# A two-layer streaming encoder on one Trainium2 core: ScalarE loads one table set for logarithm and exponential ahead of the norms of each stage

## The reference, cut to what matters

```python
def rms_norm(x, g):
    y = xf * lax.rsqrt(jnp.mean(xf * xf, axis=-1, keepdims=True) + RMS_EPS)
    return (y * g.astype(jnp.float32)).astype(x.dtype)

def layer(x, ...):
    m, ... = token_mix(rms_norm(x, ng[NORM_MIX_PRE]), ...)   # attention heads and RWKV-7 heads
    x = x + rms_norm(m, ng[NORM_MIX_POST])
    c = cross_attend(rms_norm(x, ng[NORM_X_PRE]), mem_k, mem_v, w_q, w_o)
    x = x + rms_norm(c, ng[NORM_X_POST])
    f = swiglu(rms_norm(x, ng[NORM_FFN_PRE]), w_gu, w_dn)
    x = x + rms_norm(f, ng[NORM_FFN_POST])
```

## Time and profile before

| | |
|---|---|
| median of 3 runs | 4215.57 us (4213.71 to 4216.14) |
| span of the profiled execution | 4217.2 us |
| TensorE busy | 3606.6 us (86%) |
| VectorE busy | 1806.6 us (43%) |
| ScalarE busy | 1447.4 us (34%) |
| GpSimd busy | 128.0 us (3%) |
| table loads on ScalarE | 121, of 1283 ns each |

### The profile page before, as it was taken

The page is one execution under the profiler, slowest core; times in us unless marked ns, Lnnn a source line. Parts: engine busy times, 40 slices in busy tenths (PEclk is TensorE's granted clock), DMA queues, the critical chain, the costliest instruction groups (busy, mean ns, idle before and its releaser), DMA issues. The chain is left out here.

```text
span 4217.2 us, 86503 instructions
## 1 busy us (share of the span) xinstructions
PE 3606.6 (86%) x32960; PEld 3336.0 (79%) x32960; DVE 1806.6 (43%) x2729; ACT 1447.4 (34%) x2667; POOL 128.0 (3%) x188
## 2 busy tenths in 40 slices
PE   4889779987887999999749796899688889999995
PEld 3878647766787999999749784677588789999994
DVE  3345346533654333333451453555345543333334
ACT  3334344433554111111342343444245531111115
POOL 0000000001000000000000100000001000000000
PEclk6999869887998999999979896899799899999997
DMA  5111111105641111111131112101175311111111
GB/s 170 52 55 62 61 36 42 65 23 187 210 170 36 46 45 49 45 45 45 36 107 41 59 62 61 36 25 65 36 256 212 105 36 45 45 45 47 43 50 51
DMA packets 249818, 306.36 MB, mean 73 GB/s; under 512 B 27252, under 2 KB 203844, under 8 KB 248480
## 3 DMA queue, kind: packets, MB, share of 16 engines
q1 hardware_dynamic: 232320, 225.61, 16.9%
q0 software_dynamic: 17184, 76.45, 4.8%
HBM read 231.01 MB, written 71.00 MB: 72 GB/s over the span
## 5 line engine op out<-in xcount | busy, mean ns | idle before, releaser
L779 PE MATMUL PS<-HH,WH 128*128 128x352 f32 (+3 forms) x3712 | 1240.7, 334 | 125.3 <-PEq L763 125.3
L779 PE MATMUL PS<-HH,WL 128*128 128x352 f32 (+3 forms) x3712 | 1211.8, 326 | 0.0
L779 PE MATMUL PS<-HL,WH 128*128 128x352 f32 (+3 forms) x3712 | 1209.5, 326 | 0.0
L779 PEld LDWEIGHTS PS<-HH,WH 128*128 128x128 f32 x3712 | 719.3, 194 | 147.0 <-issue 141.8
L779 PEld LDWEIGHTS PS<-HH,WL 128*128 128x128 f32 x3712 | 719.3, 194 | 3.0 <-issue 0.3
L779 PEld LDWEIGHTS PS<-HL,WH 128*128 128x128 f32 x3712 | 716.8, 193 | 0.0
L2326 DVE TENSOR_TENSOR WL<-WRAW,WH 128x1024 fp32r<-128x1024 f32 x194 | 241.2, 1243 | 659.0 <-DVEq L2325 659.0
L1515 ACT CAST WH<-WRAW 128x1024 fp32r<-128x1024 f32 x218 | 228.6, 1049 | 608.1 <-ACTq L1520 564.5
L1479 PE MATMUL PS<-GH,WH 128*128 128x352 f32 x1056 | 342.0, 324 | 0.0
L1479 PE MATMUL PS<-GH,WL 128*128 128x352 f32 x1056 | 340.9, 323 | 0.0
L1479 PE MATMUL PS<-GL,WH 128*128 128x352 f32 x1056 | 340.8, 323 | 0.0
(11 more groups left out here) (336 smaller groups left out, 4929.7 us busy)
## 6 DMA issues: line engine op xcount, KB each, us to landing
WRAW<-in_w_gate_up SPq DMA_DIRECT2D x88, 512.0 KB, 3.7
W<-split_dram SPq DMA_DIRECT2D x48, 512.0 KB, 4.5
WRAW<-in_w_down SPq DMA_DIRECT2D x46, 512.0 KB, 3.2
WH<-split_dram SPq DMA_DIRECT2D x40, 512.0 KB, 3.7
WL<-split_dram SPq DMA_DIRECT2D x40, 512.0 KB, 4.6
WRAW<-in_w_in SPq DMA_DIRECT2D x38, 512.0 KB, 3.7
raw_dram<-MIX SPq DMA_DIRECT2D x24, 528.0 KB, 3.1
R<-raw_dram SPq DMA_DIRECT2D x24, 512.0 KB, 3.5
```

Source lines behind the costliest of these rows:

```text
L779: ins = e.matmul(out, lhs(k, wp), rhs(k, xp), start=first, stop=(k == n - 1 and xp == 1))
```

## The change

ScalarE's program gets a helper that loads the set `natural_log_exp_and_others`, and calls it at six places: ahead of the memory squares, in every pair at its fourth tile pair, in the RWKV prologue behind the sigmoids, at the start of the output projection, in the first FFN half behind its first SiLU, and behind the last FFN half. Nothing else of the program is touched; which loads are put in when it is built follows from the set that is in place.

```diff
+        def roots_ahead():
+
+            e.preload_act_table_set("natural_log_exp_and_others")
+
...
             e.wait_ge(S("memT_act"), 1)
             e.sem_inc(S("memT_act"), -1)
+            roots_ahead()
             squares(R2, MEM)
             highs(in_tmp, MEM)
...
                 for n, (u, x0) in enumerate(tile_pairs(j)):
                     by_token(u, x0)
                     by_token(u, x0 + 1)
+                    if n == 3:
+                        roots_ahead()
                     if n < 3:
                         lora(ahead, 2 * n)
...
             lora(0, 0, 1, 2, 3, 4, 5)
+            roots_ahead()
             key_row(0)
             key_squares(0)
             decays(0)
...
+            roots_ahead()
             for half in range(2):
                 copy(HH[:, 4 * half:4 * half + 4, part_span(0)], R2[:, 4 * half:4 * half + 4, part_span(0)]).then_inc(S("hh_ready"), 1)
...
             def first_half():
                 silu(0)
+                roots_ahead()
                 stat(2, 2)
...
             half(0)
             half(1)
+            roots_ahead()
             squares_out(0)
```

## The result

The changed kernel takes **4169.33 us** (median of 4 runs, 4165.29 to 4172.42), the kernel before beside it 4215.85 us (4213.71 to 4223.21): ratio 0.9888, 95% interval 0.9870 to 0.9907. The forecast was 4166 us, with a range of 4144 to 4192. The profiled execution of the changed kernel took 4172.42 us, its span is 4170.8.

A forecast was written before the change was run, and what follows sets the result against it. TensorE, busy 86% of 4217.2 us, was taken as the bound; ScalarE edits pay only where TensorE waits for it. Fifteen terms summed to 24.6 us per layer, 49.2 for both, forecasting 4166 us, range 4144 to 4192.

The forecast's parts named there:

- Term 1: Memory norm: two loads go (2.6 us), an explicit one comes ahead of the first square (1.3); gain 1.3 us per layer.
- Term 9: Projection's first norm: TensorE waits 0.71 us and about as long again for banks ScalarE returns late; gain 1.3 per layer.
- term 10: Two norms around 1071 to 1081: four loads go, the copy between waits for its product; gain 3.2 us per layer.
- Term 12: Norm in the back projection: TensorE waits 3.10 us for a bank, about 1 stays; gain 2.1 us per layer.
- Term 13: Norms at 1265 and 1270: the copies between wait for products; gain 3.2 us per layer.
- term 15: Last FFN half: six loads go, one comes in an idle stretch, VectorE sets the end; gain 0.
- rival B: Shortened TensorE waits leave its clock at 2.4 GHz, each saving 1 to 3 us: 4150 us; chance 0.09.
- A: Weight transfers are late next from output projection to back projection, losing 12.4 us per layer: 4191 us; chance 0.12.
- D: Loads are still put before Ln and Exp, so the 18 explicit ones only add: 4226 us; chance 0.03.
- F: Earlier copies and casts meet VectorE or a transfer everywhere, nothing passed on: within 0.2% of 4216 us; chance 0.02.
- E: A drain behind each load exists and hides in what follows, terms twice as large: 4117 us; chance 0.02.
- C: Slower by TensorE's clock in RWKV stretches, each us at 1.2 GHz costing up to 0.46: 4295 us; chance 0.03.

The follow-up runs named there:

- experiment 5: Unedited repeats: changed kernel 4158.23 and 4161.68 us, kernel before 4222.44 us; changed kernel with each explicit load written twice, one of two kept, 4156.75 us.
- experiment 3: Changed kernel without the explicit load behind the last FFN half: 4158.09 us, ratio 0.9861 to the kernel before.
- experiments 4: Changed kernel, memory load moved to the loop's head, prologue load into the wait for the decays, projection's and pair 3's loads left out: 4156.00 us.
- experiment 6: Changed kernel with a load of the exponential's set directly ahead of every explicit load, 57 loads: 4167.62 us, ratio 0.9906 to the kernel before.
- experiment 8: Changed kernel with explicit loads moved off the path or left out, run again beside the changed kernel's third lot: 4147.58 us, ratio 0.9854 to the kernel before.
- experiment 2: Changed kernel whose explicit load at the output projection names the exponential's set, so 36 loads return through the back projection: 4195.14 us, ratio 0.9948 to the kernel before.

## Why the prediction was right, and where its steps were not

The measured time lies 3.3 us above the forecast in its own lot; over the four lots (17 runs, 4149.44 to 4172.42) the changed kernel stands at 0.9861 to 0.9888 of the kernel before, that is 4157 to 4169 by 4215.85 us. The range holds all of that, and the forecast of 4166 lies in the upper half of what was measured. The mechanism is the one forecast: 104 loads went, and the time fell where ScalarE was the late one. That the total came so near is in part luck, as the terms show: some are too large, some too small, and the clock gave and took in places where the sum had nothing.

Outside the RWKV pairs the sum had 24.6 - 0.9 - 2.5 = 21.2 us per layer, 42.4 in all; the traces show 3433.2 - 3387.1 = **46.1**. In the pairs it had 6.8; the traces show 785.9 before (mean of two, both layers) and 784.3, 769.1, 768.3 and 778.0 after: between 1.6 and 17.6. Term by term, from the matched instructions of the first traces of both kernels (first layer, then second where it differs):

| term | forecast | measured | |
|---|---|---|---|
| 1 memory norm | 1.3 | -0.3 (2.56 gained, 2.82 lost ahead of it, 0.33 of that already ahead of the first load); 1.45 (2.56, 1.11) | a load at the loop's head, exposed in the first layer |
| 2 mix norm | 2.0 | 2.1; 1.6 | |
| 3 tanh | 0 | 0 | |
| 4 RWKV prologue | 2.6 | 2.67; 2.81 | |
| 5 pair 0 | 0.9 | 0.8; 0.95 | |
| 6 pair 4 | 2.5 | 2.46 (wait 3.10 to 0.64) | |
| 7 sample norm | 2.6 | 2.56 | |
| 8 load at the projection | -1.3 | -1.28 | |
| 9 first norm | 1.3 | 0.2 | step failed |
| 10 norms in a row | 3.2 | 3.57 | |
| 11 | 2.6 | 2.56 | |
| 12 back projection | 2.1 | 2.24 of wait, 3.4 with what follows; 4.8 | clock, see below |
| 13 norms in a row | 3.2 | 4.5; 4.1 | under-sized |
| 14 first FFN half | 1.6 | 1.36 (wait 6.30 to 4.94) | |
| 15 last FFN half | 0 | 0 | but see term 1 |

The terms don't account for all of the 46.1. In the first layer 25.4 us come outside the pairs; 3.4 of them are the attention part, by the clock (experiment 5). In the second layer 21.0 come: behind term 14 the changed kernel is 49.2 us ahead, at the end of the program 46.3, and what it loses in that FFN I didn't take apart. One slip stands in the sum itself: term 10 adds 0.7 and 2.6 and writes 3.2.

**Term 9** is a step that failed. These rows of the kernel before, three of the projection and the first load of term 13, I had not weighed:

```profile
1042.04 0.33 PE L779 MATMUL PS<-HL,WH 128*128 128x384 f32 x1
...
1042.37 0.53 ACT L2033 ACTIVATE TMP<-TMP 128x384 f32<-128x384 f32 x1
...
1042.80 0.46 ACT L1515 COPY R<-PS 128x384 f32<-128x384 f32 x1
...
1265.48 1.28 ACT L2029 ACT_TABLE_LOAD   x1 [6.68 <-ACTq L2028]
```

I took the 0.71 us of TensorE's wait, "and about as long again", for ScalarE's delay, since the copy stood with no idle time behind the Exp. But the product that this copy takes out (the 128x384 of L779) ended only at 1042.37, and the copy began at 1042.80. After, where ScalarE stands idle for 2.38 us ahead of that copy, the product ends at 1032.79 and the copy starts at 1032.99, 0.20 us behind it. So ScalarE had been late by about 0.2 us of the 0.43, and that is what came: the wait fell from 0.71 to 0.50, and the next one, the "as long again" (0.65 us at 1044.80), is still 0.65. I had asked for the product's end in terms 10, 12 and 13, not here.

**Term 13** is mis-sized. I let the first of the two norms pass on 0.7 us, because the copy between would wait for its product. From the first Ln's slot to the cast before lie 9.69 us (load at 1265.48, cast at 1275.17), after 5.16 (1246.12 to 1251.28): of four loads, 5.13 us, 4.5 are passed on, 2.55 and 1.96 by the two norms. The copy between the norms now waits 0.53 us for its product, so that much is lost; I had put the loss at 1.9.

**Term 12** has its wait right (2.24 us against 2.1) but not what follows it. Behind the wait of 3.10 us TensorE soon ran at 1.2 GHz; behind the wait of 0.86 that is left it did so for a shorter time or not at all. The second layer, the kernel before and then the changed one, between the same products and VectorE instructions:

```profile
3300.40:3312.70 12.30, 10.80 (x43) 8.12 (x44) 4.66 (x7) 4.77 (x13) 0.00 (x0) 0.62 0.03 10
```

```profile
3259.30:3269.00 9.70, 7.75 (x47) 6.52 (x48) 4.25 (x7) 4.78 (x13) 0.00 (x0) 1.00 0.13 52
```

That is rival B's mechanism, at one of its waits: 2.6 us in this layer, 1.1 in the first.

**Term 1 and the loop's head.** I had bounded the load at the head by 1.3 us once and put it beside the sum. It comes in both layers (57.30 and 2102.88 us), and it comes with term 15's load: without that load it is gone, as experiment 3 shows. It stands behind ScalarE's wait, in the second layer too, where that wait is 18 us long. In the first layer the squares start 2.82 us later, of which 2.5 are both loads; in the second they start 1.11 later.

**The placement** is what experiments 4, 6 and 8 add: of the nine explicit loads per layer, four stand exposed, as the sum had them (memory, prologue, projection, first FFN half), and three of these can move or go. Taking the clock of the pairs out, that is worth another 7.2 to 11.5 us (experiment 8).

**Rivals.** A is refuted by experiment 2. D by 39 loads and none between a Ln and its Exp. F by the time itself, and by terms 6, 7 and 11, where the loads' time is passed on nearly whole. E is the drain that the Trainium skill gives in "ScalarE: Activation LUTs", section "What ACT_TABLE_LOAD costs" (1.38 us behind the load). Where one load is added and none stood before (term 8), the path steps by 1.28 us; where two go that switched between different sets (terms 7 and 11), by 2.56. With a drain these would be about 2.7 and 5.3, so it isn't there; experiment 6 agrees with its 1.29. Here the measurement decides.

B and C are one mechanism, and both signs occurred. B's side shows at term 12 and in the first layer's attention part. In the RWKV pairs the clock left 1.6 of the forecast's 6.8 us in the first trace and gave some 10 more in two others. B's rule was too strict: behind the wait of 2.93 us that ends at 1109.15 in the kernel before, the granted clock stays at 1.00. C's price was good as an upper end. In pair 2, 85.9 - 80.6 = 5.3 us are lost at a granted clock of 0.92; as 1.2 GHz counts half, that is 16% of the 85.9 us, 13.7 us at 1.2 GHz, so 0.39 us for each. In pair 1, 91.2 - 87.9 = 3.3 us are lost for 10.2 us, 0.32 for each. I had 0.46. What the runs don't bear out is that I tied these stretches to the edit alone: their length differs from execution to execution of one program.

## What to carry to other kernels

Where two functions alternate and each brings its own table load, name the one set that holds both, and put the load into idle time ahead of a wait, not behind it: in this kernel a load behind a wait cost its 1.29 us wherever other engines waited for ScalarE, and one in idle time nothing. Look at the loop's head when you change what is in place at the loop's end. Before you call an engine late because it had no idle time, look when its input was ready. And when a stage's time differs between executions of one program, judge an edit by what repeats, and look at the clock of each stage before you credit the edit with its gain.

## What the runs showed of the hardware that I had not expected

The RWKV pairs took 380.8 to 393.6 us in the first layer of one and the same program, at a granted clock of 0.91 to 0.87 of full speed, so that medians of four or five runs of it lay 12.6 us apart (4156.75 to 4169.33) while all other stages together agreed within 2.4 us, though the first layer's attention part alone took 374.2 to 378.4 us. A table load of a set already in place, with other instructions between, still takes 1.28 us (973.18 in the first trace).
